# Weight matmuls read from their last column to their first, with a shifted weight ring

## What is computed

```python
# first block
h = rms_norm(x, g_pre);  proj = h @ w_in                    # 2048 -> 6472 columns
q = rms_norm(q_lat) @ w_uq;  kv = rms_norm(kv_lat) @ w_ukv   # MLA, 8 heads; Fox attention, 8 heads
o = concat([o_mla, o_fox]) @ w_out;  x = x + rms_norm(o, g_post)
# second block
x = x + 0.5 * swiglu(rmsnorm(x), w_gate, w_up, w_down)       # 2048 -> 5632 -> 2048
x = x + hybrid_mixer(rmsnorm(x), w_in_2, ..., w_att_out, w_sg_out, w_out_2)
x = x + 0.5 * swiglu(rmsnorm(x), w_gate, w_up, w_down)
return rmsnorm(x, final_norm)
```

## Time and profile before

| | |
|---|---|
| median of two runs | 2693.69 us |
| the profiled execution's own time | 2694.18 us |
| its span, first to last instruction | 2692.4 us |
| TensorE busy | 2658.2 us (99%) |
| VectorE busy | 1430.7 us (53%) |
| ScalarE busy | 1189.7 us (44%) |
| mean granted TensorE clock | 0.996 |
| moved by DMA | 496.23 MB, 184 GB/s |

### The profile page before, as it was taken

One profiled execution on the slowest core, in us unless ns is written; L12 is line 12 of the kernel. 1 busy time (PEld: TensorE's weight loads), 2 busy tenths in 40 slices (PEclk: granted clock), 3 DMA queues, 4 the chain that ended last, 5 costly groups with the idle time before them and its releaser, 6 DMA issues.

```text
span 2692.4 us, 32506 instructions
## 1 busy us (share of the span) xinstructions
PE 2658.2 (99%) x12165; PEld 2209.8 (82%) x12165; DVE 1430.7 (53%) x1562; ACT 1189.7 (44%) x1362; POOL 27.0 (1%) x25
## 2 busy tenths in 40 slices
PE   8999999899999999999999999999999999999998
PEld 6888888788888888888888888888888888888886
DVE  6755555654545455455445655555654454544554
ACT  4544554444444443444444554444444444444333
POOL 0000000000000000000000300000000000000000
PEclk9999999999999999999999999999999999999999
DMA  6655545456565655557665445555566665565554
GB/s 196 204 161 171 158 149 194 149 185 191 188 191 188 188 188 193 190 192 232 190 195 187 147 149 180 192 191 190 185 204 190 189 189 187 187 187 194 195 188 149
DMA packets 258672, 496.23 MB, mean 184 GB/s; under 512 B 17602, under 2 KB 19992, under 8 KB 258328
## 3 DMA queue, kind: packets, MB, share of 16 engines
q1 hardware_dynamic: 257040, 489.81, 56.7%
q0 software_dynamic: 896, 4.89, 0.5%
q10 hardware_dynamic: 648, 0.32, 0.0%
HBM read 492.86 MB, written 2.10 MB: 184 GB/s over the span
## 4 chain that ended last, share of the span: by engine, by line
PE 98%; DVE 1%; DMA 0%; ACT 0%; issue 0%; ACTq 0%; DVEq 0%
PE acc L435 94%; PE tr L451 3%; PE s_ps L490 1%; PE o_ps L513 1%; DVE act_lo L1158 0%; DMA fix<-fixed 0%; PE tr L722 0%; DVE xres L1516 0%; ACT act_hi L813 0%; DVE stats L1178 0%; DVE wlo L1126 0%; DVE u L1692 0%; ACT lat L860 0%; DVE xres L1755 0%; DVE xres L1274 0%
## 5 line engine op out<-in xcount | busy, mean ns | idle before, releaser
L1126 DVE TENSOR_TENSOR wlo<-raw,whi 128x1024 fp32r<-128x1024 f32 x929 | 1135.6, 1225 | 1053.6 <-ACT whi L783 1031.1
L783 ACT ACTIVATE whi<-raw 128x1024 fp32r<-128x1024 f32 x929 | 978.9, 1057 | 1107.8 <-PE acc L435 1101.7
L435 PE MATMUL acc<-whi,act_hi 128*128 128x512 f32 (+1 forms) x2560 | 1008.3, 394 | 6.4 <-DVE wlo L1126 4.3
L435 PE MATMUL acc<-whi,act_lo 128*128 128x512 f32 (+1 forms) x2560 | 996.9, 389 | 0.0
L435 PE MATMUL acc<-wlo,act_hi 128*128 128x512 f32 (+1 forms) x2560 | 995.7, 389 | 0.0
L435 PEld LDWEIGHTS acc<-whi,act_hi 128*128 128x128 f32 x2560 | 481.9, 188 | 102.6 <-issue 5.3
L435 PEld LDWEIGHTS acc<-whi,act_lo 128*128 128x128 f32 x2560 | 481.5, 188 | 100.9
L435 PEld LDWEIGHTS acc<-wlo,act_hi 128*128 128x128 f32 x2560 | 482.2, 188 | 95.3
L435 PE MATMUL acc<-whi,h_hi 128*128 128x512 f32 x704 | 274.3, 390 | 0.0
L435 PE MATMUL acc<-whi,h_lo 128*128 128x512 f32 x704 | 274.0, 389 | 0.0
L435 PE MATMUL acc<-wlo,h_hi 128*128 128x512 f32 x704 | 273.9, 389 | 0.0
(11 more groups left out here) (217 smaller groups left out, 1302.3 us busy)
## 6 DMA issues: line engine op xcount, KB each, us to landing
raw<-in_w_in SPq DMA_DIRECT2D x280, 512.0 KB, 3.5
raw<-in_ffn_w_gate SPq DMA_DIRECT2D x176, 512.0 KB, 4.4
raw<-in_ffn_w_up SPq DMA_DIRECT2D x176, 512.0 KB, 4.2
raw<-in_ffn_w_down SPq DMA_DIRECT2D x176, 512.0 KB, 3.7
raw<-in_w_out SPq DMA_DIRECT2D x64, 512.0 KB, 4.1
raw<-in_w_sg_out SPq DMA_DIRECT2D x24, 512.0 KB, 4.6
raw<-in_w_uq SPq DMA_DIRECT2D x9, 512.0 KB, 4.1
raw<-in_w_ukv SPq DMA_DIRECT2D x8, 512.0 KB, 5.0
```

What stands on the lines that cost most here:

```text
L435: last = nc.tensor.matmul(pair[:, half, 0:width], left[:, k, tok], right[:, slot, t, 0:width], start=(k == 0 and n == 0), stop=(j == count ...
L783: nc.scalar.activation(whi[:, slot, :, 0:width], raw[:, slot, :, 0:width], ACT.Copy).then_inc(hi_ready, 1)
L1126: nc.vector.tensor_tensor(wlo[:, slot, :, 0:width], raw[:, slot, :, 0:width], whi[:, slot, :, 0:width].bitcast(F32), ALU.subtract).then_in ...
```

## The change

The moving operand and the output of each weight matmul are both indexed with step -1, from column `width - 1` to column 0, so column n of the product still lands in column n. The tiles of `whi` and `wlo` are placed 2064 bytes apart, not 2048: they begin 0, 16, ..., 112 bytes past a multiple of 512 in `whi` and, since `whi` is now 16512 bytes long, 128, 144, ..., 240 bytes past one in `wlo`. `LINE` becomes 512. `sg_lo` keeps its place relative to `region`; `merged_hi` and `merged_lo` begin 256 bytes later relative to it. `raw`, the loads, the number of instructions and the waits are as before.

```diff
-        LINE = 2048
+        LINE, STEP = 512, W + 4
...
-        whi, top = place_at("whi", [P, RING, TILES, W], F32R, top)
-        wlo, top = place_at("wlo", [P, RING, TILES, W], F32R, top)
+        whi, top = place_at("whi", [P, RING, TILES, STEP], F32R, top)
+        wlo, top = place_at("wlo", [P, RING, TILES, STEP], F32R, top)
...
-        sg_lo, top = place_at("sg_lo", [P, SG_GROUPS, SEQ], F32R, top)
-        merged_at = top
-        merged_hi, top = place_at("merged_hi", [P, KD, SEQ], F32R, top)
-        merged_lo, top = place_at("merged_lo", [P, KD, SEQ], F32R, top)
+        sg_lo, top = place_at("sg_lo", [P, SG_GROUPS, SEQ], F32R, region + SG_GROUPS * SEQ * 4)
+        merged_at = region + 2 * SG_GROUPS * SEQ * 4
+        merged_hi, top = place_at("merged_hi", [P, KD, SEQ], F32R, merged_at + 256)
+        merged_lo, top = place_at("merged_lo", [P, KD, SEQ], F32R, merged_at + 256 + KD * SEQ * 4)
...
-                                    pair[:, half, 0:width], left[:, k, tok], right[:, slot, t, 0:width],
+                                    pair[:, half, width - 1::-1], left[:, k, tok], right[:, slot, t, width - 1::-1],
```

## The result

| | median | span of the profiled execution | ratio to before (95% interval) |
|---|---|---|---|
| before | 2693.69 us | 2692.4 us | |
| changed | 2761.96 us (2761.02 to 2762.90) | 2759.2 us | 1.0254 (1.0238 to 1.0271) |

The forecast was 2611 us, faster by 3%. The change cost 68 us. The time is inside the stated range, at the place of the rival "slower: the streams meet more often" (2767 us) and not at that of the forecast.

A forecast was written before the change was run, and what follows sets the result against it. TensorE's matmul pace was taken as the bound, 11,052 weight matmuls at 226.7 ns. Saving 7.5 ns on each gave 2694.2 - 83 = 2611 us; other parts cost nothing. Range 2564 to 2770 us.

The forecast's parts named there:

- slower: the streams meet more often: Every weight matmul: opposite streams cross and the pace never settles, 233.3 ns, +73 us, 2767 us; chance 0.19.
- The bound, the count and the pace: TensorE bounds the kernel: 11,052 weight matmuls of 512 columns at 226.7 ns take 2505 us of 2694.
- What the 13.3 ns are: Excess per weight matmul over 213.3 ns, 147 us in all, read as the stationary load's read meeting the moving read.
- Constant in width: The charge is per matmul, not per column: 13.3 ns at 512 columns, 13.7 in the narrow unit of 328.
- two thirds of the 11.3 ns go: Reversal and shifted starts together save 7.5 ns on each of 11,052 weight matmuls, 83 us; faster by over 2%: 0.41.
- the best bound: Weight matmuls' excess falls to what the half-rate score matmuls pay, pace 215 to 215.4 ns, gaining 125 us.
- the settling rows: Trace rows after the scores: weight matmul distances start at 233.3 ns, average 231 over nine, then 227.
- Nothing happens: Rival: the charge comes from the port or request order, blind to addresses; 2694 us within 2%; chance 0.34.
- the rule of two independent ports: Skill's rule: stationary and moving operands use separate read ports, so there is no meeting to avoid; gain 0 us.
- Half rate: Rival: a descending operand is not streamed at full rate, 426.7 ns a matmul, +2210 us, 4904 us; chance 0.06.
- Splits, `LINE`, `merged`, supply: Ring writes in two rows, moved `merged` and load supply at faster pace: nothing added or late; `merged` 3 us, in doubt.

The follow-up runs named there:

- e5: Kernel before with only the moving operand read from last column to first, output written ascending; 2762.44 us, ratio 1.0255.
- e6: Kernel before with only the output written from last column to first; 2693.79 us, ratio 1.0001.
- e8: Kernel before with one column of the moving tile read 512 times (product of that column only); 2574.67 us, one run.
- e19: Kernel before with all stationary operands of the weight matmuls 64 bytes past a multiple of 512, ring tiles and `raw` unmoved, ascending; 2761.95 us, one run.
- e11: Kernel before with ring and all activation tensors 64 bytes later, ascending; 2693.98 us, one run.
- e9: Kernel before with 32 tokens of the stationary operand in every weight matmul, three quarters of the output rows left out; 2741.02 us, one run.
- e1: Kernel before with moving operand and output both reversed, every address as before; 2762.11 us, ratio 1.0257.
- e10: Kernel before with the tiles of `whi` and `wlo` all 64 bytes later, columns ascending; 2713.66 us, one run.
- e16: Kernel before with the tiles of `whi` and `wlo` all 32 bytes later, `LINE` 512, columns ascending; 2761.04 us, one run.

## Why the prediction was wrong, step by step

- **The bound, the count and the pace: right.** 11,052 matmuls, 226.7 ns before, and a change of pace that shows in full: 6.2 ns in the mean gave 68 us.
- **What the 13.3 ns are: partly right.** A charge on the read side (e5, e6, e8), absent at 1.2 GHz (the earlier trace rows and the 425 ns above), dependent for ascending reads on how the moving stream stands to the stationary one (e19, e11). Wrong was the reading as a meeting whose cost follows what the load reads: a quarter of the load left the charge and made the pace of the wide matmuls worse (e9). "Constant in width" does not hold for the descending read: in e1 the narrow unit takes 4.35 us for 29 distances, 150.0 ns, where the earlier trace rows had 150.3, while the wide matmuls went from 226.7 to 233.3. Its descending read also begins at another place, 1308 bytes into the tile and not 2044, so width and place cannot be told apart here.
- **The failed step: "two thirds of the 11.3 ns go".** I took the common start at a multiple of 512 bytes as the thing that makes the streams meet, hence any other start and direction as relief, and set the value nearer to the best bound. The runs show the opposite order: the common start is the best of the starts tried (226.7 against 228.8 to 233.3), and a descending read has a mean of 233.3 ns at every start tried. The term of the sum that was wrong, in sign too, is the 7.5 ns a matmul, -83 us: it measured 6.7 ns the other way in the settled pace, 6.2 in the mean, +68 us. The evidence for a good direction was one-sided: the settling rows showed that phase matters, and all their unsettled distances were longer on average than the settled one. That was noted under the rival and not weighed. Read afterwards, a pace that settles from above says that the settled state is better than the states around it. The slow state does not behave so: in e1 the twelve distances from 294.17 to 296.97 us, which begin with the third weight matmul after a block of scores, already have the mean of 233.3 ns.
- **The rival "the streams meet more often": right in sign, pace and price** (233.3 ns, 2767 us for 2762), wrong in its picture. It had the pace never settle; the reversed stream settles within a few matmuls, at 233 and 234 ns (e1). The stagger does make the pace uneven, 230 to 240 ns in the changed kernel, but leaves that mean where it is, and alone it costs less (231.2 ns). That streams in opposite directions cross, as the rival had it, no run shows.
- **"Nothing happens" and the rule of two independent ports:** refuted for this kernel. The Trainium skill (TensorE: Matmul & The Clock Gate, Part 2) has the rule that the load does not take bandwidth from the running matmul. For these fp32r matmuls it does not hold in the sense that matters here: with the moving tiles untouched, the place of the stationary operand alone changed the pace from 226.7 to 233.3 ns.
- **"Half rate": refuted.** A descending SBUF read costs 3% and a descending PSUM write nothing (e6).
- **Splits, `LINE`, `merged`, supply: right, at zero.** The splits take 1229 and 1059 ns as before; TensorE waited 4.2 us for low parts.

What stays open: how the two reads take turns, why a shorter or repeated load makes the pace of the wide matmuls worse, and why the descending read keeps its mean whatever its start. That the reversal of the moving read is the whole loss is shown (e1, e5, e6); why it costs 6.7 ns is not. All starts tried are multiples of 16 bytes, and for the descending read only the common ones at 0 and 64 and the changed kernel's mixed ones. Whether a descending load with a descending moving read would restore 226.7 ns was not measured.

## What to carry to other kernels

Where TensorE is the bound and nothing waits, take the distance of matmul starts from the timeline and compare it with columns over clock; here the constant remainder of 13.3 ns was worth 147 us, more than any wait of TensorE in the list. With a full-rate fp32r moving operand, keep moving tiles and stationary tiles at the same place modulo 256 bytes, the best of the places tried here, and read ascending: 64 bytes of padding before one of them cost 20 us (e10) or 69 us (e19), and neither shows in the list of waits. When a steady state is reached from worse ones, do not price an unknown perturbation as a gain: put the nearest rows, which are the unsettled ones, first.

## What the runs showed of the hardware that was not expected

- Addresses alone move the time of this kernel from 2693 to 2762 us, with the same instructions: the stationary operands 64 bytes later (e19), or the ring 32 bytes later (e16).
- A repeated moving column runs at 216.3 ns, a streamed one at 226.7 to 233.3 (e8 and the table).
- Loads of 32 stationary columns take 109 ns for 188, and the matmuls of 512 columns around them 231.7 ns for 226.7, those of 328 columns 146.8 for 150.3 (e9).
- The descending read has the same mean at all starts tried while its single distances differ by up to 10 ns, in a sequence that repeats with the ring (changed kernel).
- The output's direction and the alternation of PSUM banks between matmuls that accumulate change nothing that can be measured (1.0001, 0.9990 to 1.0012, for e6).
